# Two-layer MoE block on one Trainium2 core: routing the second layer's tokens block by block

## What is computed

```python
def post_norm(x, y, g, b):
    return layer_norm(DEEPNORM_ALPHA * x + y.astype(x.dtype), g, b)

def hier_moe(x, w_group, b_group, w_router, b_router, w_gate, w_up, w_down):
    xf = x.reshape(B * S, D)
    probs_g = jax.nn.softmax((xf @ w_group + b_group).astype(jnp.float32), axis=-1)
    p_top, g_idx = lax.top_k(probs_g, 1)
    logits_e = (xf @ w_router + b_router).astype(jnp.float32).reshape(T, N_GROUPS, EXPERTS_PER_GROUP)
    in_group = jnp.take_along_axis(logits_e, g_idx[:, :, None], axis=1)[:, 0]
    probs_in = jax.nn.softmax(in_group, axis=-1)
    w_top, e_local = lax.top_k(probs_in, TOP_K_IN_GROUP)
    w_top = w_top / jnp.sum(w_top, axis=-1, keepdims=True)
    ids = g_idx * EXPERTS_PER_GROUP + e_local
    gates = jnp.einsum('tk,tke->te', p_top * w_top, jax.nn.one_hot(ids, N_EXPERTS, dtype=jnp.float32))
    h = jax.nn.silu(jnp.einsum('td,edf->tef', xf, w_gate)) * jnp.einsum('td,edf->tef', xf, w_up)
    y = jnp.einsum('tef,efd->td', h * gates[:, :, None].astype(h.dtype), w_down)
    return y.reshape(B, S, D)

    # in first_block, for each of the two layers:
        x = post_norm(x, mixed @ w_o[layer], ln_mix_g[layer], ln_mix_b[layer])
        moe_out = hier_moe(x, w_group[layer], ...)
        x = post_norm(x, moe_out, ln_ffn_g[layer], ln_ffn_b[layer])
```

## Time and profile before

| | us |
|---|---|
| median of 3 runs | 889.35 |
| lowest and highest | 886.92, 889.40 |
| the profiled execution | 891.08 |
| its span | 889.3 |
| PE busy | 879.4 (99%) |
| PE loading weights | 667.4 (75%) |
| DVE busy | 495.2 (56%) |
| ACT busy | 406.3 (46%) |
| POOL busy | 31.9 (4%) |

### The profile page before, as it was taken

One profiled execution on the slowest core, in us unless ns is written; L12 is line 12 of the kernel. 1 busy time (PEld: TensorE's weight loads), 2 busy tenths in 40 slices (PEclk: granted clock), 3 DMA queues, 4 the chain that ended last, 5 costly groups with the idle time before them and its releaser, 6 DMA issues.

```text
span 889.3 us, 13288 instructions
## 1 busy us (share of the span) xinstructions
PE 879.4 (99%) x5275; PEld 667.4 (75%) x5275; DVE 495.2 (56%) x758; ACT 406.3 (46%) x563; POOL 31.9 (4%) x73
## 2 busy tenths in 40 slices
PE   8999999999999999999999999999999999999998
PEld 8988998944543699878445436898878888888887
DVE  4798877712121765526221217566568777767566
ACT  5755654332221636652322215445637555556431
POOL 6100010000000000000000000000000000000010
PEclk9999999999999999999999999999999999999999
DMA  9743418869999594339599994753644555547711
GB/s 347 255 161 123 143 48 289 326 242 409 409 410 404 166 322 149 120 117 361 180 411 409 409 403 159 235 168 123 209 142 143 189 189 189 189 142 239 239 42 48
DMA packets 98222, 205.80 MB, mean 231 GB/s; under 512 B 6897, under 2 KB 51697, under 8 KB 98161
## 3 DMA queue, kind: packets, MB, share of 16 engines
q1 hardware_dynamic: 96576, 202.14, 63.0%
q10 hardware_dynamic: 1584, 2.81, 0.9%
HBM read 203.87 MB, written 1.05 MB: 230 GB/s over the span
## 4 chain that ended last, share of the span: by engine, by line
PE 88%; DVE 7%; ACT 2%; issue 2%; POOL 0%; DVEq 0%; POOLq 0%
PE psum L732 85%; DVE w_lo L2327 2%; ACT arena L1764 1%; PE psum L856 1%; PE psum L875 1%; ACT w_hi L1764 1%; PE psum L1306 0%; PE psum L999 0%; PE psum L1619 0%; DVE arena L2456 0%; DVE arena L2476 0%; PE psum L866 0%; DVE stats L2639 0%; DVE arena L2420 0%; ACT L1764 0%
## 5 line engine op out<-in xcount | busy, mean ns | idle before, releaser
L732 PE MATMUL psum<-xt,w_hi 128*128 128x256 f32 (+1 forms) x1056 | 250.9, 323 | 2.2 <-ACT w_hi L1764 1.4
L2327 DVE TENSOR_TENSOR w_lo<-raw,w_hi 128x2048 fp32r<-128x2048 f32 x86 | 196.0, 2287 | 41.6 <-ACT w_hi L1764 41.4
L732 PE MATMUL psum<-xt,w_lo 128*128 128x256 f32 x704 | 191.6, 282 | 0.0
L732 PEld LDWEIGHTS psum<-xt,w_hi 128*128 128x128 f32 x1056 | 174.2, 190 | 19.8 <-issue 3.4
L1764 ACT ACTIVATE w_hi<-raw 128x2048 fp32r<-128x2048 f32 (+1 forms) x92 | 169.6, 1853 | 30.3 <-PE psum L732 20.9
L732 PEld LDWEIGHTS psum<-xt,w_lo 128*128 128x128 f32 x704 | 131.0, 190 | 0.0
L732 PE MATMUL psum<-w_hi,xt 128*128 128x512 f32 (+1 forms) x336 | 104.0, 380 | 0.6 <-DVE w_lo L2327 0.4
L1764 ACT ACTIVATE arena<-psum 128x512 f32<-128x512 f32 (+2 forms) x74 | 43.5, 602 | 116.3 <-PE psum L732 85.1
L732 PE MATMUL psum<-hi_as_raw,x_slots 128*64 128x512 f32 x176 | 81.2, 597 | 0.0
L732 PE MATMUL psum<-lo_as_raw,x_slots 128*64 128x512 f32 x176 | 81.2, 597 | 0.0
L732 PEld LDWEIGHTS psum<-w_hi,xt 128*128 128x128 f32 x336 | 61.3, 189 | 12.5 <-issue 1.8
(11 more groups left out here) (273 smaller groups left out, 1263.2 us busy)
## 6 DMA issues: line engine op xcount, KB each, us to landing
hi_as_raw<-in_gate_up SPq DMA_DIRECT2D x44, 512.0 KB, 9.3
lo_as_raw<-in_gate_up SPq DMA_DIRECT2D x44, 512.0 KB, 10.9
raw<-in_ffn_w_up SPq DMA_DIRECT2D x44, 512.0 KB, 4.5
raw<-in_gate_up SPq DMA_DIRECT2D x40, 512.0 KB, 7.7
raw<-in_w_down SPq DMA_DIRECT2D x24, 512.0 KB, 12.4
raw<-in_attn_w_in SPq DMA_DIRECT2D x24, 512.0 KB, 5.6
raw<-in_ffn_w_down SPq DMA_DIRECT2D x22, 512.0 KB, 4.1
hi_as_raw<-in_w_down SPq DMA_DIRECT2D x20, 512.0 KB, 12.7
```

Of the source, the lines that this page charges most:

```text
L732: return pe.matmul(o, l, r, start=start, stop=stop, skip_group_check=skip)
L2327: return dve.tensor_tensor(w_half(h, w_lo), w_half(h, raw), w_half(h, w_hi).bitcast(F32), ALU.subtract).then_inc(lo_split, 1)
```

## The change

In the second layer:

- PE counts block 0 between the two halves of block 1's turn, and signals counted for it. DVE then works out block 0's slots (slots_at) and its slot matrix before it takes up block 1's logits. PE gathers block 0's chunks 4 to 7 ahead of the second count, chunks 3, 1 and 0 behind it and behind three fillers (there were five and five), and chunk 2 once the counts have been read.
- Block 1's norm goes by halves of the columns on DVE: shift half 0, scale half 1, the slot matrix, rest of half 0, shift half 1, rest of half 1. Its scaling of half 0 comes behind its choice.

In both layers block 1's gather takes four chunks at a time, first the rounded parts, then the rests, each behind its own signal (x_rounded, x_rest for each half). The number of gathers stays at 32. Before, the first pair of chunks was complete after 4 matmuls of block 1, now after 6; the others after 8, 14 and 16 (before 8, 12 and 16).

```diff
@@ -1144,7 +1144,9 @@
                     ch = r_chosen[:, 0:EXPERTS]
                     mm(psum[:, 6, 0:16], before[:], ch, True, False, skip=True)
                     for n in range(2):
-                        mm(psum[:, 6, 16 + 16 * n:32 + 16 * n], ones[:], ch, False, False, skip=True)
+                        last = mm(psum[:, 6, 16 + 16 * n:32 + 16 * n], ones[:], ch, False, False, skip=True)
+                    if layer:
+                        last.then_inc(sem("counted"), 1)
 
                 def count_second():
 
@@ -1166,18 +1168,6 @@
                     if share == 8 / 16:
                         count_second()
 
-                if layer == 0:
-                    fm_half("MK1", mt_hi, mt_lo, between)
-                else:
-                    turn_raw(1, 1)
-                    raw_logits(1, 1)
-                    count_first()
-                    keep_busy(5, 7)
-                    count_second()
-                    keep_busy(5, 7)
-                pe.wait_ge(sem("placed"), layer + 1)
-                load = pe.value_load(load_max[0:1, 0:1], min_val=0, max_val=T)
-
                 def gather_block(g, r, bank, b):
 
                     for k in range(2 * r, 2 * r + 2):
@@ -1194,17 +1184,28 @@
                     for b in range(TB):
                         gather_block(g, r, bank, b)
 
-                def gather_first(b):
-
-                    pe.wait_ge(s["perm_ready"], b + 1)
-                    for k, bank in enumerate(FIRST_BANKS):
-                        if layer == 0 and b == 0 and bank == 7:
+                def gather_first(ks):
+
+                    for k in ks:
+                        bank = FIRST_BANKS[k]
+                        if layer == 0 and bank == 7:
                             pe.wait_ge(drained_a, drained_by("MK1", "a"))
                         for x in (x_hi, x_lo):
-                            last = mm(psum[:, bank, :], x[:, b, P * k:P * k + P], perm_both[:, :, b, :],
-                                      b == 0 and x is x_hi, b == 1 and x is x_lo, skip=True)
-                        if b and k % 2:
-                            last.then_inc(s["gathered"], 1)
+                            mm(psum[:, bank, :], x[:, 0, P * k:P * k + P], perm_both[:, :, 0, :], x is x_hi, False,
+                               skip=True)
+
+                def gather_second():
+
+                    pe.wait_ge(s["perm_ready"], 2)
+                    for c in range(2):
+                        for x, ready, done_by in ((x_hi, sem("x_rounded"), 3 * layer + 2 + c),
+                                                  (x_lo, sem("x_rest"), 3 * layer + 2 + c)):
+                            pe.wait_ge(ready, done_by)
+                            for k in range(4 * c, 4 * c + 4):
+                                last = mm(psum[:, FIRST_BANKS[k], :], x[:, 1, P * k:P * k + P], perm_both[:, :, 1, :],
+                                          False, x is x_lo, skip=True)
+                                if x is x_lo and k % 2:
+                                    last.then_inc(s["gathered"], 1)
 
                 def gather_two(p):
 
@@ -1426,9 +1427,28 @@
                     for c in range(2):
                         turn_part(turn_set, norm_no, 0, c)
 
-                for b in range(TB):
-                    pe.wait_ge(sem("x_rest"), 2 * layer + b + 1)
-                    gather_first(b)
+                if layer == 0:
+                    fm_half("MK1", mt_hi, mt_lo, between)
+                    pe.wait_ge(sem("placed"), 1)
+                    load = pe.value_load(load_max[0:1, 0:1], min_val=0, max_val=T)
+                    pe.wait_ge(sem("x_rest"), 1)
+                    pe.wait_ge(s["perm_ready"], 1)
+                    gather_first(range(KC))
+                else:
+                    turn_raw(1, 1, (0,))
+                    count_first()
+                    turn_raw(1, 1, (1,))
+                    raw_logits(1, 1)
+                    pe.wait_ge(sem("x_rest"), 4)
+                    pe.wait_ge(s["perm_ready"], 1)
+                    gather_first(range(4, 8))
+                    count_second()
+                    keep_busy(3, 7)
+                    gather_first((3, 1, 0))
+                    pe.wait_ge(sem("placed"), 2)
+                    load = pe.value_load(load_max[0:1, 0:1], min_val=0, max_val=T)
+                    gather_first((2,))
+                gather_second()
                 with pe.If(load > FAST_LIMIT):
                     dense_path()
                 with pe.Else():
@@ -2715,10 +2735,10 @@
                     own.did(dve.scalar_tensor_tensor(x_res[:, b, cs], x_res[:, b, cs], mv[:, b, 0:1], gain[:, 0, cs],
                                                      ALU.subtract, ALU.mult))
 
-                def shift(b):
+                def shift(b, halves=range(2)):
                     dve.wait_ge(rstd_ready, 3 + 2 * n + b + 1)
                     own.settle()
-                    for c in range(2):
+                    for c in halves:
                         cs = slice(512 * c, 512 * c + 512)
                         dve.scalar_tensor_tensor(x_res[:, b, cs], x_res[:, b, cs], rstd[:, b:b + 1], gain[:, 1, cs],
                                                  ALU.mult, ALU.add).then_inc(ln_done, 1)
@@ -2735,12 +2755,11 @@
                     dve.wait_ge(sem("x_rounded"), 3 * layer + 1)
                     rest(x_lo[:, 0, :], x_res[:, 0, :], x_hi[:, 0, :]).then_inc(sem("x_rest"), 1)
 
-                def rest_second():
-                    for c in range(2):
+                def rest_second(halves=range(2)):
+                    for c in halves:
                         cs = slice(512 * c, 512 * c + 512)
                         dve.wait_ge(sem("x_rounded"), 3 * layer + 2 + c)
-                        last = rest(x_lo[:, 1, cs], x_res[:, 1, cs], x_hi[:, 1, cs])
-                    last.then_inc(sem("x_rest"), 1)
+                        rest(x_lo[:, 1, cs], x_res[:, 1, cs], x_hi[:, 1, cs]).then_inc(sem("x_rest"), 1)
 
                 split_to(h + (6, 5)[layer])
                 for c in range(2):
@@ -2761,17 +2780,34 @@
                     rest_first()
                 measure(1, 1)
                 gather_stats(1)
-                scale(1, 0)
-                logits(1)
-                choose(1)
                 if layer == 0:
+                    scale(1, 0)
+                    logits(1)
+                    choose(1)
                     rest_first()
-                scale(1, 1)
-                count_slots(layer)
-                place_first(layer, 0)
-                shift(1)
-                place_first(layer, 1)
-                rest_second()
+                    scale(1, 1)
+                    count_slots()
+                    place_first(layer, 0)
+                    shift(1)
+                    place_first(layer, 1)
+                    rest_second()
+                else:
+                    dve.wait_ge(sem("counted"), 3)
+                    slots_at(0)
+                    place_first(layer, 0)
+                    logits(1)
+                    choose(1)
+                    scale(1, 0)
+                    dve.wait_ge(sem("counted"), 4)
+                    slots_at(1)
+                    own.settle()
+                    most_slots()
+                    shift(1, (0,))
+                    scale(1, 1)
+                    place_first(layer, 1)
+                    rest_second((0,))
+                    shift(1, (1,))
+                    rest_second((1,))
                 less_top()
 
             def choose(b):
@@ -2794,12 +2830,21 @@
                 dve.scalar_tensor_tensor(r_chosen[:, 16 * b:16 * b + 16].rearrange("p (g e) -> p g e", e=4),
                                          rank[:, 1:5, :], 2.0, mask, ALU.is_lt, ALU.mult).then_inc(sem("chosen"), 1)
 
-            def count_slots(layer):
-
-                dve.wait_ge(sem("counted"), 2 * layer + 1)
+            def most_slots():
                 dve.tensor_reduce(load_max[:], psum[:, 6, 32:48], AX, ALU.max).then_inc(sem("placed"), 1)
+
+            def slots_at(b):
+
+                own.link(dve.scalar_tensor_tensor(r_at[:, b, :], psum[:, 6, 16 * b:16 * b + 16], 1.0,
+                                                  r_chosen[:, 16 * b:16 * b + 16], ALU.add, ALU.mult))
+
+            def count_slots():
+
+                dve.wait_ge(sem("counted"), 1)
+                most_slots()
                 own.link(dve.scalar_tensor_tensor(r_at.rearrange("p b e -> p (b e)"), psum[:, 6, 0:32], 1.0,
                                                   r_chosen, ALU.add, ALU.mult))
+
             def less_top():
 
                 own.link(dve.tensor_reduce(r_top, r_fours, AX, ALU.max))
```

## The result

| | before | changed |
|---|---|---|
| median of the 22 runs of each, us | 889.38 | 891.93 |
| lowest and highest, us | 886.86 to 891.43 | 889.0 to 894.13 |
| profiled execution: span, us | 889.3 | 891.0 |
| first turn of block 1's raw rows, second layer (T) | 413.98 | 413.26 |
| TensorE's first expert rows | T + 14.61 | T + 15.51 |

The changed kernel is slower: the ratio is 1.0027, with a 95% interval of 1.0017 to 1.0036. The prediction was 888.2 us, a gain of 1.1; it is a loss of 2.5. By the prediction's own mark (0.3% is what a measurement tells from no change) that would still be "same", but with 22 runs of each the interval leaves no change out.

A forecast was written before the change was run, and what follows sets the result against it. It took PE's matmul stream to bound most of the kernel, with PE's and the gates' chains nearly tied in the second layer's routing. Terms -1.58 and +0.46 gave -1.1, from 889.35 to 888.2 us; range 885.8 to 890.3.

The forecast's parts named there:

- The step that failed: Second layer, PE: gather over at 426.3, 12 expert rows directly behind it until 428.9, then about 0.8 us of waiting.
- The gates' chain: Second layer, DVE and ACT: copies start at 424.4 instead of 425.98, gates at 429.8 instead of 431.37, gain 1.58 us.
- PE's chain: Second layer: block 1's gather over at 426.3 instead of 428.59, a gain of 2.3 us on PE alone.
- Moving the first count, the transposes and the load of the maximum: Second layer: logits end at 417.6 instead of 417.28, block 1's choice 0.06 us later, load at nothing (0.5 if late).
- The first layer: Block 1's gather order there delays ACT's copies, exponential and gates by two gathers: loss 0.46 us, between 0 and 0.47.
- Slower, by the clock: Rival, chance 0.13: narrow matmuls from 414.0 to 417.5 lower the second layer's clock, at most 1.9 us more, 890.1 us.
- Some 15 us to spare: Expert stage, second layer: refilled weights, first used at 456.46, arrive some 15 us before they are needed.
- the case of a loss: Whole kernel: the outcome slower by about 0.3% (2.7 us) or more, given a chance of 0.04.

The follow-up runs named there:

- experiment 6: Kernel before the change, with one wait for ACT's first pair of copies added on PE ahead of the second layer's jump; 891.98 us, ratio 1.0026.
- experiment 2: Changed kernel with nine multiplications by zero on PE ahead of the second layer's jump, behind a wait for ACT's first copies; 889.99 us, ratio 1.0013.
- experiment 3: Changed kernel with the first layer's gather of block 1 back in its old order; 891.15 us, ratio 1.0021.
- experiment 1: PE's jump between the expert paths taken out in the second layer, in both kernels: changed kernel 888.0 us (0.9985), kernel before 889.41 us (1.0006).

## Why the prediction was wrong, point by point

**The step that failed** is that of PE in the second layer, where it says "PE will wait there for about 0.8 us, since its 12 rows end at 426.3 + 2.6 = 428.9". It lets the expert rows follow the gather directly, at 426.3. Measured, TensorE stood still for 2.60 us ahead of them. Between gather and rows stands a jump, which the prediction did not cost at all, though both lists of TensorE's order end in it. Its cover before the change was work queued behind the last wait, from 424.12 to 428.59, 4.5 us. The change took 3.1 us of that away: 424.76 to 426.17 is 1.4. The step of the working that should have asked is the one on the covers: an operation at no cost must be named with the work that hides it, and here the operation itself was missing.

**The gates' chain** was foretold well, if somewhat too early: -1.58, measured -1.28 wherever the jump is out of the way (T + 16.11). The difference begins on DVE, which idles 0.28 us between the maximum and the first shift, and what stands behind it is 0.3 to 0.4 us later (exponential at T + 14.56 instead of T + 14.25). PE's wait ahead of the gates is 0.47 and not 0.8.

**PE's chain** by itself, foretold as -2.3, is -1.77 (expert rows from T + 14.61 to T + 12.84): the gather starts when block 1's slot matrix is made, at T + 8.90, where I had T + 8.52.

**Moving the first count, the transposes and the load of the maximum** cost nothing, as said. Logits, choice and load stand where they were forecast within 0.1 us (logits over at T + 3.59, forecast T + 3.62).

**The first layer** lost 0.46 to 0.48 us, as worked out. That jump is covered: the q8 packet comes at 179.0, the gathers last until 182.2. It was the best step of the prediction and the smallest term.

**Slower, by the clock**, the rival at 890.1, had the right sign and the wrong place. The narrow matmuls from 413 to 418 did no harm, the clock is 1.00 there in the changed kernel as before. They may be followed by a low clock in single executions: experiment 6's, with the old order of that stretch, had 0.50 from 420 to 426. In the changed kernel it fell behind the hole, over the expert rows, and cost 1.5 us in the profiled execution (the twelve rows and the way to the gates, 4.29 us instead of 2.78). The rule of the Trainium skill that the prediction cites (TensorE: Matmul & The Clock Gate, Part 1), that activity releases the clock, agrees with this place: what preceded the 0.50 was TensorE's 2.6 us without work, and with all but 0.87 us of them filled the clock stayed at 1.00 (experiment 2).

**The sum as it should have been:** first layer +0.46; expert rows +0.90 (T + 15.51 for T + 14.61); low clock +1.51. That makes +2.87 for an execution in which the clock falls. Where it holds it is +0.46 + 0.90 = +1.4 with this hole, and +0.46 + 0.26 = +0.7 with the shorter one of experiment 3. The medians differ by 2.55, and by the mean clocks it was low at some place in 21 of the 22 runs. The gates' gain of 1.28 isn't in this sum, because the gates waited for TensorE.

**"Some 15 us to spare"** for the refilled weights holds for the first refills only. In experiment 1's kernel made from the one before, TensorE waited for the last w_down of the stage, 0.15 and 1.06 us, in its profiled execution:

```profile
531.80 0.61 PE L732 MATMUL psum<-hi_as_raw,ht 128*64 128x512 f32 x1 [1.06 <-DMA lo_as_raw<-in_w_down]
```

That changed no verdict, but a shift isn't carried to the end one to one in every execution.

**The range**, 885.8 to 890.3, was too narrow, since the missing operation has no bound in it. Even with the jump seen and no duration at hand, the rows would have given 0 to 4.5 us (all of the cover it had), and the case of a loss would have had more than 4 in 100.

## What to carry to other kernels

Look for the taken branches in an engine's stream, and for the last wait ahead of each: what counts is the work queued between that wait and the jump, 3.6 to 4.4 us of it here, and not whether the engine looks busy. A change that shortens the stream ahead of a jump, or makes its last wait later, shortens this cover, and its gain stops there; and the standstill can bring a low clock on top, 1.5 us more behind 2.60 us of it here. Look also at what a run's time is made of behind the change: a stage that the edit doesn't touch moved single times by 2.3 us. If the order can be chosen, let the last inputs arrive together and early rather than in halves, one of which is late.
